# Two-layer block in fp32, batch 1, 256 tokens: three of eight steps of the second MLP's down product as seven block products

## The reference

```python
u = rmsnorm(x, g_mlp) @ w_up
return x + jnp.square(jax.nn.relu(u)) @ w_down
```

## Time and profile before

| | us |
|---|---|
| median of three runs | 2705.34 |
| lowest, highest | 2705.13, 2705.54 |
| the profiled execution, its own time | 2704.91 |
| its span, first to last instruction | 2702.9 |
| TensorE busy | 2691.9 |
| VectorE busy | 1706.4 |
| ScalarE busy | 1297.1 |
| granted TensorE clock, mean | 1.000 |

### The profile page before, as it was taken

The page is one execution under the profiler, slowest core; times in us unless marked ns, Lnnn a source line. Parts: engine busy times, 40 slices in busy tenths (PEclk is TensorE's granted clock), DMA queues, the critical chain, the costliest instruction groups (busy, mean ns, idle before and its releaser), DMA issues.

```text
span 2702.9 us, 39959 instructions
## 1 busy us (share of the span) xinstructions
PE 2691.9 (100%) x13676; PEld 2274.4 (84%) x13676; DVE 1706.4 (63%) x2422; ACT 1297.1 (48%) x1790; POOL 23.2 (1%) x52
## 2 busy tenths in 40 slices
PE   9999999999999999999999999999999999999999
PEld 7888888888888888888888888888888888888887
DVE  5687776555555655655656667878776565565564
ACT  5455555444444544444434554556454344443443
POOL 0100000000000000000000000000000000000000
PEclk9999999999999999999999999999999999999999
DMA  7655556666665555555555555544455555555555
GB/s 271 227 174 179 191 169 196 204 197 197 204 208 186 186 187 193 185 193 191 188 193 184 191 181 168 167 157 154 152 184 187 194 187 190 191 186 194 188 187 171
DMA packets 140605, 508.86 MB, mean 188 GB/s; under 512 B 15942, under 2 KB 16231, under 8 KB 140232
## 3 DMA queue, kind: packets, MB, share of 16 engines
q1 hardware_dynamic: 136312, 493.86, 55.2%
q0 software_dynamic: 2736, 10.75, 1.2%
q10 hardware_dynamic: 1440, 2.62, 0.3%
HBM read 502.98 MB, written 4.19 MB: 188 GB/s over the span
## 4 chain that ended last, share of the span: by engine, by line
PE 97%; DVE 2%; DMA 1%; ACT 1%; issue 0%; SPq 0%; ACTq 0%; DVEq 0%
PE acc L1709 25%; PE acc L1710 13%; PE acc L1724 5%; PE pS L1741 4%; PE pS L1743 4%; PE pS L1742 4%; PE pT L1741 4%; PE pT L1743 4%; PE pT L1742 4%; PE acc L1741 4%; PE acc L1743 3%; PE acc L1742 3%; PE pO L1741 2%; PE pO L1742 2%; PE pO L1743 2%; PE pG L1741 2%
## 5 line engine op out<-in xcount | busy, mean ns | idle before, releaser
L1001 DVE TENSOR_TENSOR wlo<-raw,whi 128x1024 fp32r<-128x1024 f32 x938 | 1146.6, 1224 | 753.1 <-ACT whi L536 749.3
L536 ACT ACTIVATE whi<-raw 128x1024 fp32r<-128x1024 f32 x938 | 991.6, 1058 | 929.0 <-PE pT L1743 342.4
L1709 PE MATMUL acc<-a_w,whi 128*128 128x512 f32 x2944 | 1046.2, 400 | 0.1
L1710 PE MATMUL acc<-a_w,wlo 128*128 128x256 f32 x2944 | 826.7, 281 | 0.0
L1709 PEld LDWEIGHTS acc<-a_w,whi 128*128 128x128 f32 x2944 | 553.2, 188 | 138.5 <-issue 0.8
L1710 PEld LDWEIGHTS acc<-a_w,wlo 128*128 128x128 f32 x2944 | 556.1, 189 | 0.7
L1724 PE MATMUL acc<-a_w,whi 128*128 128x512 f32 x592 | 214.9, 404 | 0.0
L1725 PE MATMUL acc<-a_w,wlo 128*128 128x256 f32 x592 | 165.8, 280 | 0.0
L739 ACT ACTIVATE t<-acc 128x256 f32<-128x256 f32 x128 | 49.2, 385 | 234.8 <-PE acc L1710 234.8
L1318 DVE TENSOR_TENSOR t<-acc,t 128x256 f32<-128x256 f32 x128 | 54.4, 425 | 125.4 <-ACT t L739 125.3
L1724 PEld LDWEIGHTS acc<-a_w,whi 128*128 128x128 f32 x592 | 111.2, 188 | 26.5 <-issue 1.8
(11 more groups left out here) (417 smaller groups left out, 3411.7 us busy)
## 6 DMA issues: line engine op xcount, KB each, us to landing
raw<-stream SPq DMA_DIRECT2D x938, 512.0 KB, 3.3
gbias<-gateb POOLq DMA_DIRECT2D x12, 256.0 KB, 3.5
X<-x_rows POOLq DMA_DIRECT2D x1, 2048.0 KB, 10.8
bias_scratch<-brow POOLq DMA_DIRECT2D x8, 256.0 KB, 5.6
out<-X ACTq DMA_DIRECT2D x8, 256.0 KB, 4.4
xF<-x SPq DMA_DIRECT2D x6, 256.0 KB, 6.5
bias<-bias_scratch POOLq DMA_DIRECT2D x8, 128.0 KB, 3.9
wg<-gates POOLq DMA_DIRECT2D x8, 128.0 KB, 4.2
```

What stands on the lines that cost most here:

```text
L536: A(whi[:, slot, :], raw[:, slot, :], ACT.Copy).then_inc(s.hi_done, 1)
L1001: TT(wlo[:, slot, :], raw[:, slot, :], whi[:, slot, :].bitcast(F32), SUB).then_inc(s.lo_done, 1)
L1709: MM(ps, wh, wide[:, k0 + k, :], start=start and k == 0, stop=False, skip_group_check=True)
L1710: last = MM(ps[:, 0:T], wl, wide[:, k0 + k, 0:T], start=False, stop=not start and k == KC - 1, skip_group_check=True)
```

## The change

In the second MLP's down product the column blocks are taken in pairs (q = 0, 1), and their chunks come by turns: chunk c+2t holds step t of column block 2q, chunk c+2t+1 the same step of block 2q+1. The stream is laid out for it, and the eight steps of hidden channels come in the order 0, 3, 1, 4, 2, 5, 6, 7 (`STEP_ORDER`). A step is a product of a 2 by 2 arrangement of blocks (two token halves, two tiles of hidden channels; two tiles, two column blocks).

- Steps t = 0, 2, 4 of each pair (`QUICK`) are done with seven block products (`quick_step`, 21 matmuls of 512 columns) in place of eight (24). Four of the seven use sums of weight blocks: VectorE makes them (`weight_sums`, three instructions), ScalarE rounds all four at once (`sums_hi`, 128 by 2048), VectorE takes the rest (`sums_lo`, 128 by 2048). Of the pair's second chunk only half is split. Four use sums of hidden tiles (`mixed_tiles`, in the up product). `weight_sums` waits until both chunks of its step have landed. Both chunks of such a step are given back (`mm_done`) after its sixth and its seventh product.
- The parts that several blocks share stand in pV, pN, `acc[0]` and `acc[1]` over the three steps. After the third, ScalarE copies `acc[0]` to `m1`, VectorE makes four sums of 512 columns (`quick_parts`, at t = 5) and adds them into X (`quick_add`, at t = 6). At t = 7 both column blocks are added to X.
- The 20 block products of the other five steps are as before, and so is the first MLP.
- State-space part: `ssd_bc` goes. Two small products (four matmul instructions) give the running sum with heads on 16 partitions, ScalarE copies it (`crow`), POOL's queue writes it to memory and reads it back spread over 128 partitions, 256 KB for two heads, into four buffers `cumb`, where `q` lay; the first load waits for the last attention scores.
- Start: the rows of x come as four loads of 512 KB, which wait for `lo_done` of 5, 7, 9 and 11; VectorE and ScalarE prepare chunks 8 to 11 before the squares, which go behind chunks 12 to 15; the copies of the first values and the broadcast of the first norm move back by three chunks.

```diff
+QUICK = {0: 0, 2: 1, 4: 2}
+STEP_ORDER = (0, 3, 1, 4, 2, 5, 6, 7)
+QUICK_CHUNKS = {}
+for _p in range(2 * FF_GROUPS):
+    for _t, _k in QUICK.items():
+        for _e in range(2):
+            QUICK_CHUNKS[B_MLP2 + 64 * (_p // 2) + 32 + 16 * (_p % 2) + 2 * _t + _e] = (len(QUICK) * _p + _k, _e)
+
...
             nc.gpsimd.memset(L, 0.0).then_inc(s.pads, 1)
-            pool.wait_ge(x_landed[7], 16)
-            pool.dma_start(X, x_rows).then_inc(s.xtok_landed, 16)
+            for n in range(NG):
+                pool.wait_ge(s.lo_done, 5 + 2 * n)
+                pool.dma_start(X[:, :, COLS * n:COLS * n + COLS], x_rows[:, :, COLS * n:COLS * n + COLS])\
+                    .then_inc(xtok_landed[n], 16)
 
 
...
+            flat = bias_scratch[0, 0:16 * T]
+            pool.dma_start(flat.rearrange("(n t) -> n t", t=T), crow[0:16, :]).then_inc(s.crow_out, 16)
+            pool.wait_ge(s.crow_out, 16)
+            pool.wait_ge(s.scores_ready, 16)
+            for m in range(8):
+                if m >= 4:
+                    pool.wait_ge(s.ssd_exp, m - 3)
+                pool.dma_start(cumb[:, m % 4, :], flat[2 * T * m:2 * T * m + 2 * T].unsqueeze(0).to_broadcast([P, 2 * T]))\
+                    .then_inc(cumb_landed[m % 4], 16)
 
 
...
                     act.wait_ge(s.mm_done, c.value(1 - NSLOT))
+                k, second = (None, 0) if c.terms else QUICK_CHUNKS.get(c.base, (None, 0))
+                if second:
+                    A(whi[:, slot, COLS:], raw[:, slot, COLS:], ACT.Copy).then_inc(s.hi_done, 1)
+                    return
                 A(whi[:, slot, :], raw[:, slot, :], ACT.Copy).then_inc(s.hi_done, 1)
+                if k is not None:
+                    act.wait_ge(s.sums_made, k + 1)
+                    A(sums_hi[:, k % 2, :], sums, ACT.Copy).then_inc(s.sums_hi, 1)
 
             def norm_in(m, gain):
...
+
+                    def down_pair(g, q):
+                        c, i = b + 64 * g + 32 + 16 * q, i0 + 4 * g + 2 * q
+                        for t in range(8):
+                            if t == max(QUICK) + 1:
+                                act.wait_ge(s.mm_done, c + 2 * t)
+                                if g + q:
+                                    act.wait_ge(s.m_added, 4 * (2 * g + q))
+                                apart(act)
+                                A(m1, acc[0], ACT.Copy).then_inc(s.m1_copied, 1)
+                            prep(At(c + 2 * t))
+                            prep(At(c + 2 * t + 1))
...
                         A(kibd[r, T * h:T * h + T], pT[r, 0:T], ACT.Copy, scale=pcol("g_kidx")[r]).then_inc(s.ki_ready, 1)
+                if n == 5:
+                    act.wait_ge(s.cum_ready, 1)
+                    A(crow[0:16, :], pG[0:16, 0:T], ACT.Copy).then_inc(s.crow_ready, 1)
...
                 slot = c.mod(NSLOT)
+                k, second = (None, 0) if c.terms else QUICK_CHUNKS.get(c.base, (None, 0))
+                if second:
+                    dve.wait_ge(s.sums_hi, k + 1)
+                    TT(sums_lo[:, k % 2, :], sums, sums_hi[:, k % 2, :].bitcast(F32), SUB).then_inc(s.sums_lo, 1)
+                    dve.wait_ge(s.hi_done, c.value(1))
+                    TT(wlo[:, slot, COLS:], raw[:, slot, COLS:], whi[:, slot, COLS:].bitcast(F32), SUB).then_inc(s.lo_done, 1)
+                    return
+                if k is not None:
+                    weight_sums(c.base, slot, k)
                 dve.wait_ge(s.hi_done, c.value(1))
                 TT(wlo[:, slot, :], raw[:, slot, :], whi[:, slot, :].bitcast(F32), SUB).then_inc(s.lo_done, 1)
+
+            def weight_sums(c, slot, k):
+
+                for e in range(2):
+                    dve.wait_ge(landed[slot + e], 16 * ((c + e) // NSLOT + 1))
+                if k:
+                    dve.wait_ge(s.sums_hi, k)
+                    dve.wait_ge(s.sums_lo, k)
+                b21, b22 = raw[:, slot, COLS:], raw[:, slot + 1, COLS:]
+                d1, d2, d4 = sums[:, 0:COLS], sums[:, 2 * COLS:3 * COLS], sums[:, 3 * COLS:]
+                TT(sums[:, 0:2 * COLS].rearrange("p (k c) -> p k c", k=2),
+                   raw[:, slot + 1, :].rearrange("p (k c) -> p k c", k=2), raw[:, slot:slot + 2, 0:COLS], SUB).then_inc(s.sums_step, 1)
+                dve.wait_ge(s.sums_step, 2 * k + 1)
+                TT(d2, b22, d1, SUB).then_inc(s.sums_step, 1)
+                dve.wait_ge(s.sums_step, 2 * k + 2)
+                TT(d4, b21, d2, SUB).then_inc(s.sums_made, 1)
 
...
 
-            for n in range(NG):
-                prep(At(NG + n))
+            for c in range(NG, 3 * NG):
+                prep(At(c))
             total_squares(8, 1, 1)
             rsqrt_tok(ss[:, 0, :], rT)
             dve.nop(nofuse=True).then_inc(s.rb_ready, 1)
-            for c in range(2 * NG, 16):
+            for c in range(3 * NG, 16):
                 prep(At(c))
...
 
+            def mixed_tiles(j, k):
+
+                a11, a21, a12, a22 = even[:, 0:P], even[:, P:T], t2[:, 0:P], t2[:, P:T]
+                s1, s2, s3, s4 = (mixed[:, P * e:P * e + P] for e in range(4))
+                dve.wait_ge(s.up_dve, 2 * (64 + 16 * (k // len(QUICK)) + 2 * j + 2))
+                if k:
+                    dve.wait_ge(s.mixed_ready, k)
+                TT(s1, a21, a22, ADD).then_inc(s.mixed_step, 1)
+                TT(s3, a11, a21, SUB).then_inc(s.mixed_step, 1)
+                dve.wait_ge(s.mixed_step, 3 * k + 2)
+                TT(s2, s1, a11, SUB).then_inc(s.mixed_step, 1)
+                dve.wait_ge(s.mixed_step, 3 * k + 3)
+                TT(s4, a12, s2, SUB).then_inc(s.mixed_made, 1)
+                dve.wait_ge(s.mixed_hi, k + 1)
+                TT(mixed_lo[:, j, :], mixed, mixed_hi[:, j, :].bitcast(F32), SUB).then_inc(s.mixed_ready, 1)
+
+            def quick_parts(p, c):
+
+                dve.wait_ge(s.m1_copied, p + 1)
+                dve.wait_ge(s.mm_done, c)
+                if p:
+                    dve.wait_ge(s.m_added, 4 * p)
+                TT(u2, pV, m1, ADD).then_inc(s.m_step, 1)
+                dve.wait_ge(s.m_step, 3 * p + 1)
+                TT(u3, pN, u2, ADD).then_inc(s.m_step, 1)
+                dve.wait_ge(s.m_step, 3 * p + 2)
+                TT(u2, acc[1], u2, ADD).then_inc(s.m_step, 1)
+                TT(u4, acc[1], u3, ADD).then_inc(s.m_free, 1)
+                dve.wait_ge(s.m_step, 3 * p + 3)
+                dve.wait_ge(s.m_free, p + 1)
+
+            def quick_add(n, i):
+
+                dve.wait_ge(s.t_evac, 2 * i - 4)
+                for h, e, part in ((0, 0, m1), (0, 1, u2), (1, 0, u3), (1, 1, u4)):
+                    xg = X[:, h, COLS * (n + e):COLS * (n + e) + COLS]
+                    STT(xg, part, rsq[:, h:h + 1], xg, MUL, ADD).then_inc(s.m_added, 1)
+
             def mlp(b, a, i0, layer, stage, gain):
...
+                    def down_pair(q):
+                        c, i, n = b + 64 * g + 32 + 16 * q, i0 + 4 * g + 2 * q, 2 * q
+                        for t in range(8):
+                            if t == max(QUICK) + 1:
+                                quick_parts(2 * g + q, c + 2 * t)
+                            if t == max(QUICK) + 2:
+                                quick_add(n, i)
+                            for e in range(2):
+                                if t == 7:
+                                    if e == 0:
+                                        dve.wait_ge(s.m_added, 4 * (2 * g + q) + 4)
+                                    for h in range(2):
+                                        xg = X[:, h, COLS * (n + e):COLS * (n + e) + COLS]
+                                        evac_tok(At(c + 14 + e), At(i + e), h, tbanks(At(i + e), True),
+                                                 lambda ps: STT(xg, ps, rsq[:, h:h + 1], xg, MUL, ADD))
...
 
-                dve.wait_ge(s.ssd_bc, m + 1)
+                dve.wait_ge(cumb_landed[m % 4], 16 * (m // 4 + 1))
                 if m:
                     dve.wait_ge(s.ssd_exp, m)
-                TT(em.rearrange("p (k l) -> p k l", k=4), pG.rearrange("p (k l) -> p k l", k=4),
+                TT(em.rearrange("p (k l) -> p k l", k=4), cumb[:, m % 4, :].rearrange("p (k l) -> p k l", k=4),
                    tril.unsqueeze(1).to_broadcast([P, 4, 128]), ADD).then_inc(s.ssd_em, 1)
...
 
+            def quick_step(c, k, i, first, last):
+
+                slot, t = c % NSLOT, k // len(QUICK)
+                j = k % len(QUICK)
+                pe.wait_ge(s.lo_done, c + 2)
+                pe.wait_ge(s.sums_lo, k + 1)
+                pe.wait_ge(s.mixed_ready, len(QUICK) * (t // 2) + j + 1)
+                pe.wait_ge(s.hid_ready, 64 + 16 * (t // 2) + 2 * j + 2)
+                d = [[w[:, k % 2, COLS * e:COLS * e + COLS] for w in (sums_hi, sums_lo)] for e in range(4)]
+                m = [[w[:, j, P * e:P * e + P] for w in (mixed_hi, mixed_lo)] for e in range(4)]
+                half = lambda r, h: [b_w[:, 2 * j + r, T * w + P * h:T * w + P * h + P] for w in range(2)]
```

(78 more changed lines are left out.)

94 lines of the change are left out of this document (60 added, 34 removed).

## The result

The changed kernel takes 2711.44 us (median of 12 runs, 2709.62 to 2713.59), the kernel before 2705.15 beside it (12 runs, 2703.49 to 2705.54): 1.0026 times as long, with a 95% interval of 1.0018 to 1.0034. It is slower, by 6.3 us, as forecast. The profiled execution has 2713.35 us with a span of 2711.7, 8.8 more than before.

A forecast was written before the change was run, and what follows sets the result against it. TensorE bounds the kernel, 97% of the chain. Second MLP -16.3 + 31.8 + 2.6 = +18.1, state-space part -6.7, start -2.7: +8.7 on 2704.91, 2713.6; median 2714 us, range 2700 to 2724.

The forecast's parts named there:

- the forecast's own: Whole kernel: the forecast's own band of times, 2708 to 2721 us, with a chance of 0.55.
- The chains in VectorE: Second MLP's down product: load, sums, rounding, rest wait for each other, 11.1 us between most seven-product steps, 23.16 before q1 t0.
- The bare rate: VectorE's float32 instructions: one result a cycle at 0.96 GHz, 2.13 us for 2048 columns, some 4 us less of waits.
- The waits: Second MLP: eight TensorE waits per group, at seven-product steps, `acc[0]` and pS; sum 7.95 us, x 4 = +31.8.
- the restarts: Second MLP: after each wait TensorE loses another 0.08 us at its first matmul, 4 x 8 x 0.08 = +2.6 us.
- State-space part: Eight `ssd_bc` of 0.89 us go, four instructions come back at 0.45, new loads covered: -6.7 us.
- Start: Start of the kernel: TensorE's waits of 1.41 and 1.14 us and two restarts go, -2.7 us, bounds 0 and -3.
- TensorE as the bound: Rival for the whole kernel: chains hidden, TensorE stays the bound, -25.7 us, 2679 us; chance 0.10.
- cover argument: Second MLP's down product: VectorE's 39 us a pair fit on average in TensorE's 41.5; the order doesn't fit.
- Shorter chains: Rival, second MLP: faster landing and shorter long instructions take 8 us, 2706, or 2701; 2698 to 2708, chance 0.22.
- dearer handovers: Rival: each handover costs 0.1 more, some six a step, 24 x 0.6 = +14, 2728 us; 2721 to 2735, chance 0.13.
- a clock that falls after a wait of 2 us: Second MLP: named as what would make the forecast wrong, waits of 2 us lowering the granted clock; no size given.

The follow-up runs named there:

- sums_once: The changed kernel with the sums of weight blocks made for the first two seven-product steps only and used in all (output not the reference's): 2683.53 us.
- plain_down_old_start: The changed kernel with the second MLP's down product and the start as before, so the state-space part alone: 2698.5 us.
- after (2): Second profile of the changed kernel, run once more unaltered: span 2709.8 us, median of its runs 2711.58 us.
- the first pair of runs: The changed kernel with the second MLP's down product as before, once with the changed start (2695.15 us), once with the old start (2698.5 us).
- split_and_late: The changed kernel with rounding and rest of the weight sums in halves, and q0's adds into X moved later in groups 0 to 2: 2685.72 us.
- split_rounding: The changed kernel with the rounding and the rest of the weight sums each cut in two instructions of 1024 columns: 2693.38 us.

## Why the prediction was right, step by step

The forecast was 2714.0 us, +8.7 on the profiled execution. That execution grew by 8.4 and the median by 6.3; 2711.44 lies in the range and in the forecast's own. That the profiled execution meets the forecast to 0.3 us is luck: by the stages the second MLP cost 2.2 less than forecast (15.9 against 18.1), and the start gave back 2.0 less (0.7 against 2.7), for a late chunk 0 and a fallen clock that were not in the forecast. The medians, 2.4 apart from the forecast, show the error of the sum.

**The chains in VectorE: right.** Their lengths, start to start of two seven-product steps, in group 1 of the rows above:

| from, to | measured | forecast | TensorE's own work, forecast |
|---|---|---|---|
| q0 t0 to q0 t2 | 11.29 | 11.29 | 10.20 |
| q0 t2 to q0 t4 | 11.23 | 11.13 | 10.20 |
| q0 t4 to q1 t0 | 23.25 | 23.16 | 21.08 |
| q1 t0 to q1 t2 | 12.37 | 12.42 | 10.20 |
| q1 t2 to q1 t4 | 11.06 | 11.13 | 10.20 |

Together 69.20 against 69.13. Within a chain the terms are less exact and partly cancel: for q0 t4 the start of TensorE to the issue of the load is 0.12 (0.03 forecast), issue to sums 3.49 (3.35), sums to rounding 0.04 (0.08), VectorE's last half to TensorE 0.05 (0.14). The forms that the new steps use, by their groups in the second MLP (count, busy us, mean ns, idle before):

```profile
L1088 DVE TENSOR_TENSOR sums_lo<-sums,sums_hi 128x2048 fp32r<-128x2048 f32 x24 | 55.0, 2291 | 17.0 <-ACT sums_hi L595 17.0
L1106 DVE TENSOR_TENSOR sums<-raw 128x1024 f32<-128x1024 f32 x24 | 29.3, 1222 | 10.7 <-DMA raw<-stream 5.7 <-issue 5.0
L1450 DVE SCALAR_TENSOR_TENSOR X<-u,tsm,X 128x512 f32<-128x512 f32 x24 | 16.6, 746 | 0.0
```

2.291 us for 2048 columns, 2.30 forecast; ScalarE's 1.92 above, 1.91 forecast. The bare rate that the prediction had from the Trainium skill, an estimated 2.13 for the former, misses the trace by 0.16. Another section of the same page of the Trainium skill ("VectorE: DVE Perf Modes", "The TRN2 errata") adds a fixed 151 cycles to each float32 instruction of this kind, an estimated 2.291, and the trace agrees.

**The waits: right in place, a little large in size, and by a flaw of the sum.** Forecast for a group 0.7, 0.44, 0.65, 0.93, 2.08, 0.38, 1.84, 0.93; measured 0.52, 0.29, 0.45, 0.83, 1.98, 0.22, 1.61, 0.61. The two largest are where they were said to be. The chains are right and the waits smaller, so TensorE's own side is longer than forecast. Two terms make most of that: a restart takes 0.11, not 0.08, and a seven-product step without a wait 4.84, not 4.76 (start to start of the chunk behind it, in `sums_once`). The larger restart stood in the trace of before, in the matmuls at 33.86 and 34.19 us; the prediction used the one at 27.03 and 27.34. In the rows above, matmuls with mixed tiles stand 0.23 to 0.24 apart. Both lie ahead of the next wait, which a VectorE chain ends at its own time, so they come out of that wait, save behind the last step of a group. The forecast priced the restarts a second time, +2.6 on top of waits measured against a TensorE without them. Without that term it says +15.5 for the second MLP, where +18.1 stood and +15.9 was measured.

**State-space part: right.** -6.7 forecast, -6.4 and -6.5 by the stages, 6.5 by `plain_down_old_start`. No matmul on pG stands there any more but the two small products, and the loads are covered: the first went out at 1847.8 and the first mask stood at 1860.0, without a wait, a load taking 4.0 us (8.6 was the bound).

**Start: right where the clock stays.** -2.7 forecast; -2.6 by the stages of after (2), 3.3 by the two medians of the first pair of runs, and -1.5 in the profile in which the clock fell. The waits at 27 and 34 us are gone.

**The rivals.** TensorE as the bound (2679) is false of this kernel, and nearly true of `sums_once` (2683.5) and of `split_and_late` (2685.7). Its cover argument, 39 us of VectorE work in 41.5, was right too: it fits once the order fits, as `split_rounding` and `split_and_late` show. Shorter chains (2698 to 2708) and dearer handovers (2728) fall with the table. What the forecast had named as a danger, a clock that falls after a wait of 2 us, does happen, and cost nothing in the down product (below).

## What to carry to other kernels

Fewer matmuls pay only if what feeds them stays off their path: weigh the longest chain between two uses, start to start, against the bound engine's own time in the same stretch, not busy time against busy time. Where two engines hand one block back and forth (sum, round, take the rest), cut it in halves so that both work at once, and put work that nobody waits for, such as an addition into the result, behind what the bound engine waits for. When waits are counted against such a chain, what the waiting engine loses at its restart is already in the chain.
